# Weighted adds of gathered rows in both branches ahead of the last half copy, and a last tile that is multiplied by the norm vector ahead of its root

## The chip, the cores and the metric

The kernel runs on one core of one Trainium2 chip. The metric is the device time of one execution in microseconds (us), as the median of several runs; lower is better. The core's engines work side by side, each on its own queue, and wait for each other by semaphores: PE (TensorE, matrix products), DVE (VectorE), ACT (ScalarE), POOL (GpSimd) and SP (SyncE, which only issues transfers here).

## The reference

One decoder layer over 512 positions of 1024 channels, all in float32: a mixer (forgetting attention, a gated recurrence and a convolution side by side), cross-attention over 256 memory tokens, a mixture of experts, and a final norm. The change touches only what stands behind the experts. Each token goes to two of 16 experts, with weights w1st and w2nd; their outputs are added to the residual stream, and the sum is normed:

```python
def rmsnorm(x, g):
    y = xf * lax.rsqrt(jnp.mean(xf * xf, axis=-1, keepdims=True) + EPS)
    return (y * g.astype(jnp.float32)).astype(x.dtype)
...
    x = x + hierarchical_moe(rmsnorm(x, ffn_norm_g[l]), ...)
return rmsnorm(x, final_norm_g)
```

## The kernel before

Everything is written out by hand: each engine has its own program, and the order of its instructions is that of the code. Positions stand in four tiles t of 128 rows, `x_sb[:, t, :]` being the residual stream of a tile.

**The experts.** Tokens are sorted by expert into 12 passes p of 128 rows. For each pass, POOL gathers its rows, PE turns them, multiplies by gate and up, ACT and DVE make the hidden rows, and PE multiplies down into two banks of 512 columns. Each bank is copied to `ysb` by a `y_half(p)`: ACT the first half, DVE the second (line 1168). SP stores passes 0 to 9 to `y_dram`. Passes 10 and 11 are never stored (LATE is 2).

**The way back.** A token's two rows come back by either way. If they lie in passes 0 to 9, POOL gathers them from `y_dram` into `ygath`, eight indirect transfers in the order of tile t and of k, first or second expert (line 616). On DVE, `add_row(k, t, w)` waits for its transfer and adds the gathered rows times the weight to `x_sb` (line 1217). Rows of passes 10 and 11 come through PE: `spread_late(t)` multiplies a matrix of weights by `ysb` (line 1636), two banks for each tile. The second half of each such product needs pass 11, hence both last `y_half` copies. `add_late(t)` on DVE adds the two banks to `x_sb` (line 1224).

**Overflow.** If an expert has more than 96 tokens, a flag `over` is set, and each engine enters a branch `If` that works off what is left. With these inputs it is not entered. DVE loads the flag into a register at line 1187; the `Else` is empty. Two small instructions on `posm` (lines 1185 and 1186) prepare the overflow work ahead of it.

**The end.** For each tile ACT squares `x_sb` with a running sum (line 804, "square" below), DVE turns the sum into mean plus epsilon (`last_mean`, line 1229), POOL raises it to the power -0.5 (`final_root`, line 611), DVE multiplies `x_sb` by this root and by the norm vector `fgain` into `n_sb` (`last_norm`, line 1234), and SP stores 512 KB to the output (line 564). DVE's order is: eight add_row, then for each t add_late(t), last_norm(t-1), last_mean(t), and at the end last_norm(3).

Of the kernel before, what the change touches and what calls it, by code (L numbers as in the profile page):

```python
# [10 lines left out]
ALU = mybir.AluOpType  # L11
ACT = mybir.ActivationFunctionType
# [24 lines left out]
ST = S // P  # L37
# [30 lines left out]
NP = EX * CAP // P  # L68
# [39 lines left out]
def build(nc, x, mem, mix_norm_g, w_in, fox_f_bias, fox_norm_g, hgrn_lb_logits, hgrn_norm_g,  # L108
# [3 lines left out]
    with ExitStack() as ctx:  # L112
# [3 lines left out]
        def sem(name):  # L116
            return ctx.enter_context(nc.semaphore(name))


        x_sb = sb("x_sb", [P, ST, D])  # L120
# [285 lines left out]
        fin_ms = sem("fin_ms")  # L406
        fin_root = sem("fin_root")
        fin_out = sem("fin_out")
        half_done = sem("half_done")
        xs_step = sem("xs_step")  # L410
        root_step = sem("root_step")
# [89 lines left out]
        def experts_loads(sp):  # L501
# [59 lines left out]
                pass  # L561
            for t in range(ST):
                sp.wait_ge(fin_out, t + 1)
                sp.dma_start(out[0, t * P:(t + 1) * P, :], n_sb[:, t, :]).then_inc(out_done, 16)
            sp.wait_ge(out_done, 16 * ST)

# [178 lines left out]
        def experts_act(act):  # L745
# [56 lines left out]
            for t in range(ST):  # L802
                act.wait_ge(fin_sum, 2 * ST + 2 * t + 2)
                nc.scalar.activation(n_sb[:, t, :], x_sb[:, t, :], ACT.Square, 
                                     accum_out=ss[:, NORM0[3] + ST + t:NORM0[3] + ST + t + 1]).then_inc(fin_sq, 1)


        PROJ = ([("t", cuT[:, c], ACT.Copy) for c in range(2)] + [("t", cgT[:, c], ACT.Sigmoid) for c in range(2)]
# [197 lines left out]
        def experts_dve(dve):  # L1006
# [156 lines left out]
            def y_half(p):  # L1163
                dve.wait_ge(y_ps, 2 * p + 2)
                if p >= 2:

                    dve.wait_ge(y_stored[p % 2], 16 * (p // 2))
                nc.vector.tensor_copy(ysb[:, p % 2, 512:1024], PS[6][:, :]).then_inc(y_dve, 1)

            turned_rows(0)  # L1170
            for p in range(NP):
# [8 lines left out]
                    late_rows()  # L1180
                if 3 <= p < 3 + LATE:
                    late_turned(p - 3)
            y_half(NP - 1)

            link(nc.vector.scalar_tensor_tensor(out=posm, in0=picked, scalar=-4096.0, in1=pos, op0=ALU.mult, op1=ALU.add))
            link(nc.vector.tensor_scalar(posm, posm, 4096.0 - CAP + P, None, ALU.add))
            with dve.If(dve.value_load(over[0:1, 0:1]) > 0):
                dve.wait_ge(gu_ps, NP)
                dve.wait_ge(ht_ps, NP)
                with dve.Fori(0, OVER_PARTS) as q:  # L1190

                    nc.vector.tensor_scalar(posm, posm, -float(P), None, ALU.add).then_inc(ov_pos, 1)
                    with dve.Fori(0, EX) as e:
# [13 lines left out]
                        nc.vector.tensor_tensor(hid[:, 0], sg[:, 0], PS[2][:, FF:2 * FF], ALU.mult).then_inc(ov_hid, 1)  # L1207

                        dve.wait_ge(ov_stored, 16 * k + 16)
            with dve.Else():  # L1210
                pass

            def add_row(k, t, w):
                dve.wait_ge(fin_in[t][k], 16)
                if k:
                    dve.wait_ge(fin_sum, 2 * t + 1)
                nc.vector.scalar_tensor_tensor(out=x_sb[:, t, :], in0=ygath[:, t, k, :], scalar=w[:, t:t + 1],  # L1217
                                               in1=x_sb[:, t, :], op0=ALU.mult, op1=ALU.add).then_inc(fin_sum, 1)

            def add_late(t):  # L1220
                for n in range(2):
# [4 lines left out]
            def last_mean(t):  # L1226
                f = NORM0[3] + ST + t
                dve.wait_ge(fin_sq, t + 1)
                nc.vector.tensor_scalar(ss[:, f:f + 1], ss[:, f:f + 1], 1.0 / D, EPS, ALU.mult, ALU.add).then_inc(fin_ms, 1)

            def last_norm(t):
                f = NORM0[3] + ST + t
                dve.wait_ge(fin_root, t + 1)
                nc.vector.scalar_tensor_tensor(out=n_sb[:, t, :], in0=x_sb[:, t, :], scalar=rstd[:, f:f + 1],
                                               in1=fgain, op0=ALU.mult, op1=ALU.mult).then_inc(fin_out, 1)

            for t in range(ST):
                add_row(0, t, w1st)
                add_row(1, t, w2nd)
            dve.wait_ge(fin_sum, 2 * ST)  # L1240
            dve.wait_ge(router_in, 16 * 5)
            for t in range(ST):
                add_late(t)
                if t:
                    last_norm(t - 1)
                last_mean(t)
            last_norm(ST - 1)


        @block.vector  # L1250
# [839 lines left out]
```

## Time and profile before

| what | us |
|---|---|
| median of 3 runs | 762.64 |
| lowest and highest run | 762.08 and 763.15 |
| time of the profiled execution | 754.83 |
| its span, first to last instruction | 753.1 |
| PE busy | 697.4 |
| DVE busy | 276.1 |
| ACT busy | 146.7 |
| POOL busy | 64.9 |

The span is what the trace covers; the execution's own time is 1.7 us longer. Times in the trace are counted from the span's start. The profiled execution lies 7.8 us under the median of the runs. PE is busy for 93% of the span, but in the last 15 us it has no work left.

### The profile page before, as it was taken

To read this page: it belongs to the slowest core of one execution; us is meant where nothing else is said; L and a number is where in the kernel's file an instruction comes from. 1 tells how busy PE (TensorE), PEld (TensorE's weight loads), DVE (VectorE), ACT (ScalarE), POOL (GpSimd) and SP (SyncE) were. 2 spreads that over 40 slices of the span, in tenths; PEclk is the share of its full clock that TensorE was granted. 3 is DMA by queue.
4 is the path that set the end of the run, shared out by engine and by line. 5 is a ranking of instruction groups with operands and counts; after the bars stand their busy time and mean duration, and the time that the engine had idled before them with its cause. 6 is when DMAs were issued, how large, how long until landed. Compare 5 with 4: busy or idle time off the path is not lost.

```text
span 753.1 us, 8347 instructions
## 1 busy us (share of the span) xinstructions
PE 697.4 (93%) x3388; PEld 336.5 (45%) x3388; DVE 276.1 (37%) x646; ACT 146.7 (19%) x304; POOL 64.9 (9%) x94
## 2 busy tenths in 40 slices
PE   4999999999989999999999999999955999999992
PEld 3444745454546565454444446544442333333331
DVE  5046996533043544411220005412151732112147
ACT  3100441004262333311100003300010101011112
POOL 2000090420010000000000000000001000000031
PEclk9999999989999999999999999999985999999997
DMA  8730330302221303110009603030089799999562
GB/s 311 251 111 0 113 111 1 112 1 71 98 88 29 112 1 112 52 61 1 0 0 331 215 13 112 2 131 35 29 283 303 237 351 391 376 378 394 194 224 111
DMA packets 65714, 108.21 MB, mean 144 GB/s; under 512 B 5400, under 2 KB 40460, under 8 KB 65676
## 3 DMA queue, kind: packets, MB, share of 16 engines
q1 hardware_dynamic: 62796, 97.19, 37.0%
q0 software_dynamic: 2880, 10.49, 3.8%
q8 instruction: 27, 0.44, 0.2%
q14 instruction: 11, 0.09, 0.0%
HBM read 98.23 MB, written 9.44 MB: 143 GB/s over the span
## 4 chain that ended last, share of the span: by engine, by line
PE 88%; DVE 6%; ACT 2%; DMA 2%; issue 1%; POOL 0%; DVEq 0%; SPq 0%; POOLq 0%
PE bank L1722 27%; PE bank L1980 15%; PE bank L1587 11%; PE bank L1732 8%; PE bank L1615 6%; PE bank L1754 2%; PE bank L2053 2%; PE bank L1768 2%; PE bank L2033 2%; PE bank L1569 2%; PE bank L1924 2%; PE bank L1900 1%; DVE x_sb L1217 1%; PE bank L1533 1%; PE bank L1911 1%
## 5 line engine op out<-in xcount | busy, mean ns | idle before, releaser
L1722 PE MATMUL bank<-hT,W 128*128 128x512 f32 x384 | 168.4, 598 | 1.8 <-DVE hT L998 1.8
L1722 PEld LDWEIGHTS bank<-hT,W 128*128 128x128 f32 x384 | 72.9, 192 | 93.9 <-issue 91.3
L1980 PE MATMUL bank<-W,n_sb 128*128 128x512 f32 x256 | 111.5, 593 | 0.7 <-ACT n_sb L966 0.7
L1980 PEld LDWEIGHTS bank<-W,n_sb 128*128 128x128 f32 x256 | 48.1, 190 | 59.8 <-issue 58.3
L1587 PE MATMUL bank<-W,A 128*32 128x512 f32 x528 | 72.3, 607 | 1.5 <-DVE A L1152 1.5
L1295 DVE SCALAR_TENSOR_TENSOR A<-A,pc 128x511 f32<-128x511 f32 (+29 forms) x60 | 49.4, 824 | 2.1
L1615 PE MATMUL bank<-Dn,A 128*32 128x512 f32 x384 | 43.7, 595 | 0.5 <-ACT A L772 0.5
L1587 PE MATMUL bank<-hT,A 128*32 128x512 f32 x96 | 42.3, 594 | 0.0
L646 POOL TENSOR_TENSOR rstd<-ss,mhalf 128x1 f32<-128x1 f32 x14 | 7.7, 548 | 382.8 <-DVE ss L982 382.8
L1480 DVE TENSOR_TENSOR x_sb<-x_sb,bank 128x512 f32<-128x512 f32 x16 | 11.0, 687 | 79.7 <-PE bank L1980 79.7
L1587 PEld LDWEIGHTS bank<-W,A 128*32 128x32 f32 x528 | 19.2, 112 | 42.6 <-issue 40.4
L1722 PE MATMUL bank<-Dn,W 128*128 128x256 f32 x128 | 33.0, 416 | 4.1 <-DVE A L1452 3.9
L833 ACT ACTIVATE A<-bank 128x512 f32<-128x512 f32 (+1 forms) x22 | 12.2, 556 | 112.0 <-PE bank L1722 91.9
L1161 DVE TENSOR_TENSOR A<-A,bank 128x256 f32<-128x256 f32 x12 | 5.0, 421 | 75.6 <-ACT A L765 75.5
L1722 PEld LDWEIGHTS bank<-Dn,W 128*128 128x128 f32 x128 | 26.0, 208 | 12.4 <-DVE A L1452 8.4
L1420 DVE CUSTOM_DVE_ANT_0 hT<-bank,A 128x128 f32<-128x128 f32 (+3 forms) x32 | 14.4, 487 | 43.2 <-PE bank L1902 43.1
L1732 PE MATMUL bank<-W,hT 128*128 128x512 f32 x64 | 29.9, 623 | 0.0
L1495 DVE TENSOR_REDUCE fmx<-bank 128x1 f32<-128x256 f32 x16 | 6.7, 420 | 62.4 <-PE bank L2033 62.3
L1732 PE MATMUL bank<-W,Dn 128*128 128x512 f32 x64 | 28.2, 594 | 0.0
L743 ACT ACTIVATE A<-x_sb 128x1024 f32<-128x1024 f32 x8 | 8.5, 1057 | 95.8 <-DVE x_sb L1480 95.8
L1360 DVE SCALAR_TENSOR_TENSOR states<-states,Dn,bank 128x64 f32<-128x64 f32 x64 | 18.0, 281 | 19.7 <-PE bank L1808 17.2
L765 ACT ACTIVATE A<-bank 128x256 f32<-128x256 f32 x12 | 4.6, 384 | 100.9 <-PE bank L1587 100.9
(287 smaller groups left out, 796.2 us busy)
## 6 DMA issues: line engine op xcount, KB each, us to landing
Dn<-in_w_down_dram SPq DMA_DIRECT2D x16, 1024.0 KB, 12.3
W<-in_w_gate_dram SPq DMA_DIRECT2D x11, 1024.0 KB, 6.5
W<-in_w_up_dram SPq DMA_DIRECT2D x11, 1024.0 KB, 10.6
W<-in_w_in_dram SPq DMA_DIRECT2D x5, 2048.0 KB, 8.7
W<-in_w_xkv_dram SPq DMA_DIRECT2D x4, 2048.0 KB, 8.1
y_dram<-A SPq DMA_DIRECT2D x10, 512.0 KB, 10.9
W<-in_w_out_dram SPq DMA_DIRECT2D x2, 2048.0 KB, 7.7
W<-in_w_xq_dram SPq DMA_DIRECT2D x2, 2048.0 KB, 8.4
```

What stands on the lines that cost most here:

```text
L1295: nc.vector.scalar_tensor_tensor(out=y[:, s:S], in0=a[:, 0:S - s], scalar=pc[:, r:r + 1], in1=y[:, s:S], op0=ALU.mult, op1=ALU.add).then_i ...
L1360: nc.vector.scalar_tensor_tensor(out=states[:, k + 1, :], in0=states[:, k, :], scalar=he4[:, p, k * CHUNK + CHUNK - 1:k * CHUNK + CHUNK], ...
L1569: mm = nc.tensor.transpose(PS[k][:, c * P:(c + 1) * P], src[:, b, (4 * k + c) * P:(4 * k + c + 1) * P], identf[:, :])
L1587: mm = nc.tensor.matmul(PS[2 + b][r, :], xgT[:, b, c, r], gu_at[GU_HOME[e]][:, c, :], start=c == 0, stop=c == DC - 1)
L1615: mm = nc.tensor.matmul(PS[5 + n][r, :], hidT[:, p % 2, k, r], Dn[:, DN_HOME[e], k, 512 * n:512 * n + 512], start=k == 0, stop=k == 1)
L1722: mm = nc.tensor.matmul(bank[0:w, 0:n], lhs, src[:, c, 0:n], start=c == 0, stop=c == DC - 1)
L1732: mm = nc.tensor.matmul(bank[:, 0:w], src[:, c, t * P:(t + 1) * P], W[:, slot, c, col:col + w], start=c == 0, stop=c == DC - 1)
L1754: mm = nc.tensor.matmul(bank[:, 0:IW], hT[:, c, t * P:(t + 1) * P], w_if[:, c, :], start=c == 0, stop=c == DC - 1)
L1768: mm = nc.tensor.matmul(bank[:, :], lhs, hT[:, c, :], start=c == 0, stop=c == DC - 1)
L1924: mm = nc.tensor.matmul(PS[6][64 * a:64 * a + 64, i * P:(i + 1) * P], v[:, j, h * FD:(h + 1) * FD], fpT[a][:, j * P:(j + 1) * P], start=j ...
L1980: mm = nc.tensor.matmul(PS[k % 4][:, :], src[:, c, t * P:(t + 1) * P], W[:, (n_load + n) % SLOTS, c, :], start=first and j == 0, stop=last ...
L2033: mm = nc.tensor.matmul(PS[u % 2][:, 0:M], xqT[:, 2 * h + k, t * P:(t + 1) * P], xkT[:, 2 * h + k, :], start=k == 0, stop=k == 1)
```

## The change

- The two small instructions on `posm` and the load of the flag stand right behind the copy of pass 10. The copy of pass 11 on DVE, `y_half(NP - 1)`, moves into both branches.
- The eight `add_row` move into both branches. In the branch without overflow, those of tile 0 stand ahead of the copy of pass 11, the six others behind it.
- The tail's order is add_late(t), last_mean(t-1), last_norm(t-2). For the last tile, DVE first multiplies `x_sb` by `fgain` into `x_gain`, a part of `A` whose gathered rows are used up, without waiting for the root. When the root is there, DVE multiplies the first 512 columns by it, and ACT the last 512 (a copy with a scale).
- SP waits for both halves before it stores the last tile. The number of stores stays four.

```diff
--- before.py
+++ after.py
@@ -406,6 +406,8 @@
         fin_ms = sem("fin_ms")
         fin_root = sem("fin_root")
         fin_out = sem("fin_out")
+        fin_gain = sem("fin_gain")
+        fin_act = sem("fin_act")
         half_done = sem("half_done")
         xs_step = sem("xs_step")
         root_step = sem("root_step")
@@ -561,6 +563,8 @@
                 pass
             for t in range(ST):
                 sp.wait_ge(fin_out, t + 1)
+                if t == ST - 1:
+                    sp.wait_ge(fin_act, 1)
                 sp.dma_start(out[0, t * P:(t + 1) * P, :], n_sb[:, t, :]).then_inc(out_done, 16)
             sp.wait_ge(out_done, 16 * ST)
 
@@ -803,6 +807,11 @@
                 act.wait_ge(fin_sum, 2 * ST + 2 * t + 2)
                 nc.scalar.activation(n_sb[:, t, :], x_sb[:, t, :], ACT.Square, 
                                      accum_out=ss[:, NORM0[3] + ST + t:NORM0[3] + ST + t + 1]).then_inc(fin_sq, 1)
+            f = NORM0[3] + ST + t
+            act.wait_ge(fin_gain, 1)
+            act.wait_ge(fin_root, ST)
+            act.wait_ge(fin_sq, ST)
+            nc.scalar.activation(n_sb[:, t, 512:1024], A[:, 512:1024], ACT.Copy, scale=rstd[:, f:f + 1]).then_inc(fin_act, 1)
 
 
         PROJ = ([("t", cuT[:, c], ACT.Copy) for c in range(2)] + [("t", cgT[:, c], ACT.Sigmoid) for c in range(2)]
@@ -1180,11 +1189,18 @@
                     late_rows()
                 if 3 <= p < 3 + LATE:
                     late_turned(p - 3)
-            y_half(NP - 1)
+
+            def add_row(k, t, w):
+                dve.wait_ge(fin_in[t][k], 16)
+                if k:
+                    dve.wait_ge(fin_sum, 2 * t + 1)
+                nc.vector.scalar_tensor_tensor(out=x_sb[:, t, :], in0=ygath[:, t, k, :], scalar=w[:, t:t + 1],
+                                               in1=x_sb[:, t, :], op0=ALU.mult, op1=ALU.add).then_inc(fin_sum, 1)
 
             link(nc.vector.scalar_tensor_tensor(out=posm, in0=picked, scalar=-4096.0, in1=pos, op0=ALU.mult, op1=ALU.add))
             link(nc.vector.tensor_scalar(posm, posm, 4096.0 - CAP + P, None, ALU.add))
             with dve.If(dve.value_load(over[0:1, 0:1]) > 0):
+                y_half(NP - 1)
                 dve.wait_ge(gu_ps, NP)
                 dve.wait_ge(ht_ps, NP)
                 with dve.Fori(0, OVER_PARTS) as q:
@@ -1207,15 +1223,16 @@
                         nc.vector.tensor_tensor(hid[:, 0], sg[:, 0], PS[2][:, FF:2 * FF], ALU.mult).then_inc(ov_hid, 1)
 
                         dve.wait_ge(ov_stored, 16 * k + 16)
+                for t in range(ST):
+                    add_row(0, t, w1st)
+                    add_row(1, t, w2nd)
             with dve.Else():
-                pass
-
-            def add_row(k, t, w):
-                dve.wait_ge(fin_in[t][k], 16)
-                if k:
-                    dve.wait_ge(fin_sum, 2 * t + 1)
-                nc.vector.scalar_tensor_tensor(out=x_sb[:, t, :], in0=ygath[:, t, k, :], scalar=w[:, t:t + 1],
-                                               in1=x_sb[:, t, :], op0=ALU.mult, op1=ALU.add).then_inc(fin_sum, 1)
+
+                for t in range(ST):
+                    add_row(0, t, w1st)
+                    add_row(1, t, w2nd)
+                    if t == 0:
+                        y_half(NP - 1)
 
             def add_late(t):
                 for n in range(2):
@@ -1234,17 +1251,23 @@
                 nc.vector.scalar_tensor_tensor(out=n_sb[:, t, :], in0=x_sb[:, t, :], scalar=rstd[:, f:f + 1],
                                                in1=fgain, op0=ALU.mult, op1=ALU.mult).then_inc(fin_out, 1)
 
-            for t in range(ST):
-                add_row(0, t, w1st)
-                add_row(1, t, w2nd)
             dve.wait_ge(fin_sum, 2 * ST)
             dve.wait_ge(router_in, 16 * 5)
             for t in range(ST):
                 add_late(t)
                 if t:
-                    last_norm(t - 1)
-                last_mean(t)
-            last_norm(ST - 1)
+                    last_mean(t - 1)
+                if t >= 2:
+                    last_norm(t - 2)
+            x_gain = A[:, 0:1024]
+            dve.wait_ge(fin_sum, 4 * ST)
+            nc.vector.tensor_tensor(x_gain, x_sb[:, t, :], fgain, ALU.mult).then_inc(fin_gain, 1)
+            last_mean(t)
+            last_norm(t - 1)
+            dve.wait_ge(fin_gain, 1)
+            dve.wait_ge(fin_root, ST)
+            f = NORM0[3] + ST + t
+            nc.vector.tensor_scalar(n_sb[:, t, 0:512], x_gain[:, 0:512], rstd[:, f:f + 1], None, ALU.mult).then_inc(fin_out, 1)
 
 
         @block.vector
```

DVE's program, from the copies of the last two passes to the first instruction inside the overflow branch; `bank6` is the bank of the second half, TENSOR_LOAD is the flag's load. Before:

```order
L1168 COPY A<-bank6 128x512 x2
L1185 SCALAR_TENSOR_TENSOR A<-A 128x64
L1186 TENSOR_SCALAR A<-A 128x64
L1187 TENSOR_LOAD A
L1187 COMPARE_AND_BRANCH
```

Now:

```order
L1177 COPY A<-bank6 128x512
L1200 SCALAR_TENSOR_TENSOR A<-A 128x64
L1201 TENSOR_SCALAR A<-A 128x64
L1202 TENSOR_LOAD A
L1202 COMPARE_AND_BRANCH
L1177 COPY A<-bank6 128x512
```

Only one copy is left ahead of the load; the other stands first in the overflow branch here (the row behind the branch), and once more in the other branch. The next rows are DVE's again, from the end of the overflow branch to the first late add (bank0). Before:

```order
L1190 REGISTER_ALU
L1190 COMPARE_AND_BRANCH
L1187 UNCONDITIONAL_BRANCH
L1217 SCALAR_TENSOR_TENSOR x_sb<-W,A,x_sb 128x1024 x8
L1224 TENSOR_TENSOR x_sb<-x_sb,bank0 128x512
```

Now:

```order
L1197 SCALAR_TENSOR_TENSOR x_sb<-W,A,x_sb 128x1024 x8
L1202 UNCONDITIONAL_BRANCH
L1197 SCALAR_TENSOR_TENSOR x_sb<-W,A,x_sb 128x1024 x2
L1177 COPY A<-bank6 128x512
L1197 SCALAR_TENSOR_TENSOR x_sb<-W,A,x_sb 128x1024 x6
L1229 UNCONDITIONAL_BRANCH
L1241 TENSOR_TENSOR x_sb<-x_sb,bank0 128x512
```

The eight adds of the first row belong to the overflow branch. Without overflow the program goes on behind the first unconditional branch: two adds, the copy, six adds, and one more unconditional branch. Last, DVE's end, from the late adds of tile 2 (bank4 and bank7) on. Before:

```order
L1224 TENSOR_TENSOR x_sb<-x_sb,bank4 128x512
L1224 TENSOR_TENSOR x_sb<-x_sb,bank7 128x512
L1234 SCALAR_TENSOR_TENSOR n_sb<-x_sb,rstd,A 128x1024
L1229 TENSOR_SCALAR ss<-ss 128x1
L1224 TENSOR_TENSOR x_sb<-x_sb,bank5 128x512
L1224 TENSOR_TENSOR x_sb<-x_sb,bank6 128x512
L1234 SCALAR_TENSOR_TENSOR n_sb<-x_sb,rstd,A 128x1024
L1229 TENSOR_SCALAR ss<-ss 128x1
L1234 SCALAR_TENSOR_TENSOR n_sb<-x_sb,rstd,A 128x1024
```

Now, from the late adds of tile 2 on:

```order
L1241 TENSOR_TENSOR x_sb<-x_sb,bank4 128x512
L1241 TENSOR_TENSOR x_sb<-x_sb,bank7 128x512
L1246 TENSOR_SCALAR ss<-ss 128x1
L1251 SCALAR_TENSOR_TENSOR n_sb<-x_sb,rstd,A 128x1024
L1241 TENSOR_TENSOR x_sb<-x_sb,bank5 128x512
L1241 TENSOR_TENSOR x_sb<-x_sb,bank6 128x512
L1246 TENSOR_SCALAR ss<-ss 128x1
L1251 SCALAR_TENSOR_TENSOR n_sb<-x_sb,rstd,A 128x1024
L1264 TENSOR_TENSOR A<-x_sb,A 128x1024
L1246 TENSOR_SCALAR ss<-ss 128x1
L1251 SCALAR_TENSOR_TENSOR n_sb<-x_sb,rstd,A 128x1024
L1270 TENSOR_SCALAR n_sb<-A,rstd 128x512
```

Each mean and norm stands one tile later than before, and the last norm of 128x1024 has become a product of 128x1024 ahead of the last mean and a half product of 128x512 at the very end.

## Rows read from the trace of the kernel before

**Rows 1.** The page: busy tenths in 40 slices; shares of the chain.
```profile
PE   4999999999989999999999999999955999999992
DVE  5046996533043544411220005412151732112147
...
PE 88%; DVE 6%; ACT 2%; DMA 2%; issue 1%; POOL 0%; DVEq 0%; SPq 0%; POOLq 0%
```

**Rows 2.** DVE's timeline: start us, length us, line, operation [idle before <- releaser].
```profile
720.90 0.69 DVE L1168 COPY A<-bank 128x512 f32<-128x512 f32 x1 [2.60 <-PE bank L1615]
725.39 0.69 DVE L1168 COPY A<-bank 128x512 f32<-128x512 f32 x1 [3.79 <-PE bank L1615]
...
727.29 10.44 DVE L1217 SCALAR_TENSOR_TENSOR x_sb<-W,A,x_sb 128x1024 f32<-128x1024 f32 x8 [0.85 <-DVE A L1186]
737.76 1.29 DVE L1224 TENSOR_TENSOR x_sb<-x_sb,bank 128x512 f32<-128x512 f32 x2
740.26 0.15 DVE L1229 TENSOR_SCALAR ss<-ss 128x1 f32<-128x1 f32 x1 [1.21 <-ACT n_sb L804]
...
745.45 1.27 DVE L1224 TENSOR_TENSOR x_sb<-x_sb,bank 128x512 f32<-128x512 f32 x2
746.64 1.28 DVE L1234 SCALAR_TENSOR_TENSOR n_sb<-x_sb,rstd,A 128x1024 f32<-128x1024 f32 x1
747.94 0.15 DVE L1229 TENSOR_SCALAR ss<-ss 128x1 f32<-128x1 f32 x1
748.75 1.28 DVE L1234 SCALAR_TENSOR_TENSOR n_sb<-x_sb,rstd,A 128x1024 f32<-128x1024 f32 x1 [0.66 <-POOL rstd L611]
```

**Rows 3.** The chain of waits, its branch: start us, length us, what.
```profile
727.05 0.07 DVEq L1187
```

**Rows 4.** PE's late product in the timeline, and one window with the granted clock.
```profile
725.25 14.09 PE L1636 MATMUL bank<-A 128*128 128x512 f32 x32
...
727.00:738.00 11.00, 11.00 (x27) 4.86 (x26) 10.25 (x9) 0.00 (x0) 0.00 (x0) 1.00 0.12 50
```

**Rows 5.** POOL's gathers, first and last of eight; their landing; DMA at 728.
```profile
714.29 0.94 POOL L616 DMA_INDIRECT W<-y_dram,A  x1 [30.56 <-DMA y_dram<-A]
...
722.99 0.93 POOL L616 DMA_INDIRECT W<-y_dram,A  x1 [0.30 <-issue]
...
DMA to landing us min/median/max: 5.6/7.4/7.5
...
728.00:729.00 1.00, 1.00 (x4) 0.50 (x3) 0.89 (x2) 0.00 (x0) 0.00 (x0) 1.00 0.29 115
```

**Rows 6.** Timeline, two small adds on DVE, and POOL's indirect issue.
```profile
596.59 0.23 DVE L1120 TENSOR_TENSOR A<-A 128x64 f32<-128x64 f32 x1
...
597.36 0.23 DVE L1123 TENSOR_TENSOR A<-A 128x64 f32<-128x64 f32 x1
...
596.80 0.94 POOL L606 DMA_INDIRECT A<-n_dram,A  x1 [8.31 <-PE bank L1569]
```

**Rows 7.** Groups by shape: busy us, mean ns of one.
```profile
L1429 DVE TENSOR_SCALAR hT<-hT,frr 128x512 f32<-128x512 f32 x8 | 3.9, 486 | 0.3
...
L1137 DVE TENSOR_TENSOR states<-states,A 128x512 f32<-128x512 f32 x2 | 1.4, 692 | 0.1
...
L914 ACT ACTIVATE A<-n_sb 128x512 f32<-128x512 f32 x4 | 2.5, 616 | 7.6 <-DVE n_sb L1441 7.6
```

**Rows 8.** The stores of the output: issues on SP, and their landing.
```profile
L564 SPq DMA_DIRECT2D out_dram<-n_sb x4: 332/332/333, 742.8 to 750.1; - x4
...
DMA to landing us min/median/max: 2.6/2.6/2.6
```

**Rows 9.** Windows after the last store's issue; DMA share and GB/s stand last.
```profile
750.07:750.85 0.78, 0.00 (x0) 0.00 (x0) 0.00 (x0) 0.00 (x0) 0.00 (x0) 0.50 0.01 0
750.85:752.25 1.40, 0.00 (x0) 0.00 (x0) 0.00 (x0) 0.00 (x0) 0.00 (x0) 0.50 0.92 375
```

## The prediction

> **What bounds the kernel now.** I read the page's chain of work first: 88% of it is PE, 6% is DVE [rows 1]. So a change on DVE can count only where DVE ends the chain, and the slices show one such place: the last fortieth (18.8 us), where PE falls to 2 tenths and DVE rises to 7. Next the timeline of DVE over that stretch [rows 2]. It reads as one string. The copy of pass 10 starts at 720.90 and lasts 0.69; then DVE is idle for 3.79 us until PE's last down product lets the copy of pass 11 start at 725.39; 1.90 us after it the first weighted add starts (727.29), eight adds take 10.44 (2.61 for a pair), the first two late adds start at 737.76, and from there to the last norm at 748.75 DVE stands still twice, 1.21 us for the first square and 0.66 us for the last root. The reader is to see the hole of 3.79 us in front of 10.44 us of adds, and that these adds lie in the chain. The 1.90 us hold the copy, two tiny instructions, the load of the flag, and a branch that starts at 727.05, takes 0.07 and is followed by the add 0.17 us later [rows 2, 3].
>
> Then what DVE could have been waiting for. PE's late product runs from 725.25 for 14.09 us, to 739.34, at a granted clock of 1.00, that is 2.4 GHz [rows 4]; the late adds start only at 737.76, and the very last of them, second of the two from 745.45, starts at about 746.05 [rows 2], so PE has slack of 6.7 us. The gathers are issued by POOL from 714.29 to 722.99 and land 5.6 to 7.5 us later; DMA's share is down to 0.29 at 728 to 729, so the last has landed by 729 [rows 5]. The first landed at 719.9 (714.29 + 5.6, the shortest), at the latest 721.8 (with 7.5); the second was issued 1.24 later, so at the latest 723.0. Two of them lie ready while DVE is idle.
>
> **Part 1, two adds into the hole.** In the new order the tiny instructions, the flag and the branch come behind the copy of pass 10, so the first add starts at 720.90 + 1.90 = 722.80, its rows being there. The pair takes 2.61: the last copy can start at 725.41, against 725.39 before. That is nothing for PE, which waits for this copy ahead of the second half of its late product: I move PE's end from 739.34 to 739.4. The six other adds start 0.61 after the copy and take 6 x 1.305 = 7.83: they end at 725.41 + 0.61 + 7.83 = 733.85, not at 737.73. Their rows: with 7.5 us to land, rows 3 and 4 are there by 725.5 (needed at 726.0 and 727.3), 5 and 6 by 728.0 (728.6, 729.9), 7 and 8 by 730.5 (731.2, 732.6). Margins are 0.5 us and more by this worst case, so I cost the gathers at nothing. The adds save 3.9 us.
>
> **Part 2, the jump behind the adds.** The branch "no overflow" now has a body, and its end jumps to the very next instruction. No unconditional jump shows in the trace. From below it costs nothing; from above I take a whole DMA, 2.6 us from issue to landing [rows 8], as if the instructions had to be fetched. The nearest row is the taken branch: 0.07 and 0.17 behind it [rows 3]. I take 0.15: the late adds start at 734.00. The Trainium skill (Runtime: NRT & Kernel Launch, Instruction fetch mechanics) says that a taken branch stalls when its target lies outside the two instruction pages held. By that rule a stall is possible at both jumps; the row here shows that a jump over 30 instructions of DVE's program did not stall, and the new ones go 44 and 1 forward.
>
> **Part 3, the new order of the last tiles.** I follow DVE with the steps of rows 2: two late adds 1.19 (745.45 to 746.64), a mean 0.07 when its square is there, a norm 1.20 when the next does not wait for it (1.28 less the overlap of 0.08), 1.30 up to a mean behind it (746.64 to 747.94); a square's mean comes 1.18 after the square starts (the first late adds end at 737.76 + 1.29 = 739.05, the square follows them by 0.03, its mean starts at 740.26).
> - Late adds 0 at 734.00, 1 at 735.19; mean 0 waits for its square: 735.32 + 1.18 = 736.50. Late adds 2 at 736.57, mean 1 at 737.76, norm 0 at 737.83.
> - Late adds 3 at 739.03, the second of them at 739.63. PE is done at 739.4: the slack that was 6.7 us is now 0.2 us. Mean 2 at 740.22, norm 1 at 740.29.
> - The product with the norm vector at 741.49. Its form, a tensor_tensor of 128x1024 from SBUF, is not in the trace: 128x512 took 0.692 [rows 7], twice that is 1.38; the three-operand form of that size took 1.28 [rows 2]. It is nearest to the second, and I take 1.30 to the next start (bounds 1.2 and 1.4). Mean 3 needs the square of tile 3 by then: 740.25 + 1.21 = 741.5, there in time.
> - Mean 3 at 742.79, its root ready 0.81 later (747.94 to 748.75 before) at 743.60, hidden by norm 2 at 742.86 to 744.14. Then the last half: 128x512 with a scalar from SBUF took 0.486 [rows 7]; the end is 744.14 + 0.49 = 744.6 (0.07 less if the overlap holds). ACT's half starts when the root is ready and takes 0.616 [rows 7], over at 744.25, so it hides.
> DVE ended at 748.75 + 1.28 = 750.03 before. The sum on DVE is -5.4 us.
>
> **Part 4, the stores collide.** Before, the four stores followed norms 2.5 us apart and each landed 2.6 us after its issue. A store moves its data in about 1.3 us (0.92 of 1.40 us) after 0.8 us with no traffic, and lands about 0.5 us after the data [rows 8, 9]. Now the third is issued at 744.17, the fourth at 744.65. The third's data go from 744.97 to 746.27, the fourth's behind it to 747.57, landing at 748.1, not 744.65 + 2.6 = 747.25. Bounds: 0 and 0.85 us given back; the share of 0.92 says that one store fills the engines, so I take 0.85. The last landing moves from 750.07 + 2.6 = 752.67 to 748.1: **-4.6 us**.
>
> Sum: span 753.1 - 4.6 = 748.5, the profiled execution 754.83 - 4.6 = 750.3. The median of the runs is 7.8 us above that execution; nothing in the trace says where, so I carry the difference over: 762.64 - 4.6 = **758.1**. Its own range, by the bounds: 757.0 (stores do not collide, jump free, product 1.2) to 759.3 (product 1.4, jump 0.24, and a us of gathers or of PE).
>
> **Rivals.**
> - *Instruction fetch at the jumps.* For it: the trace has no unconditional jump inside these streams, and both jumps are on DVE's string. Against: rows 3. Price 2.6 us for one: 760.7; both, 763.3. Chance 8% for one, 2% for both.
> - *POOL holds the port.* The first adds read two operands from SBUF at 722.80, while POOL still issues gathers until 723.92 [rows 5]. If one had to wait, the add would start 1.12 us late and push the copy, PE and the rest by as much: 759.2. Against: a tensor_tensor with two SBUF inputs took 0.23 at 596.59 and 0.23 at 597.36, the second inside an indirect issue at 596.80 to 597.74 [rows 6]. Chance 4%. The Trainium skill (SBUF — State Buffer, Who interferes with whom) says that such a DVE instruction contends with a GpSimd one that reads SBUF; by that the time would be 759.2, and the rows of the small ones speak against it here.
> - *The rows of tile 0 come late.* The copy of pass 11 is now queued behind two adds that wait for gathers, and PE behind the copy. The second add wants its rows at 724.1; if they landed 2.6 us after that, at 726.7, everything would come 2.6 us later: 760.7. Their latest landing here is 723.0, so they would have to be 3.7 us later than in this trace. In executions of 762 us, transfers may be later than in this one. Chance 4%.
> - *PE becomes the bound, the one that ends slower.* Slack is 0.2 us now. Late by x, PE costs the new order x - 0.2, the old one only x - 6.7. Past x = 4.8 the new order loses, and past x = 6.7 its tail behind the last late add decides: 744.6 - 739.63 = 4.97 against 750.03 - 746.05 = 3.98 us, and 0.85 for the stores, so +1.8 us: 764.5. It takes a late product of over 20 us in place of 14.09, a clock near 1.2 GHz for half of it. Rows 4 have 1.00 throughout. Chance 3%.
> - *The change does not do what it says:* the adds still start behind the copy because the flag's load waits for something else. In rows 2 and 3 nothing but the 1.90 us lies between copy and add, and the flag was written long before. Then part 3 and 4 stand alone, 758.1 + 3.9 = 762.0. Chance 2%.
>
> **How the numbers follow.** The cases above leave 77% to the forecast. A difference under 0.2% (1.5 us) is about what a measurement of this kernel can't tell from none. Faster: the forecast, the port, late rows, one fetch, 93%, of which I keep back 5% for what the unexplained 7.8 us may hide: 0.88. Same: both fetches, no effect, part of what I kept back: 0.08. Slower: PE and the remainder: 0.04. The range of 8 in 10 starts at the lower bound of the forecast, 757.0, and reaches to one fetch or late rows, 760.7.
>
> **What the new profile would show.** First add near 722.8, copy of pass 11 within 0.1 us of 725.4, PE's late product of 14.1 us ending near 739.4; DVE's late adds from 734.0, hardly a gap up to 744.6; the last two stores 0.5 us apart with the last landing over 3 us after its issue. It is wrong if DVE stands idle behind either jump, if the first add or the copy starts over 0.5 us late, or if PE releases the last late add.

## The result and the profile after

The changed kernel takes 756.7 us in the median (752.91 to 759.51, 20 runs). The kernel before, run again beside it, takes 761.84 us (757.71 to 765.66, 20 runs, the first three among them), so those three, at 762.64, had been a little high. The ratio is 0.9934, with a 95% interval of 0.9919 to 0.995: 5.0 us less, between 3.8 and 6.2. The ratios here and below are worked out over the runs and lie up to 0.23% from the quotient of the two medians. The 4.6 us of the sum lie in that interval. The predicted time does not hold: 756.7 is 0.3 us below the range of 757.0 to 760.7.

The profiled execution of the changed kernel took 759.51 us, its span 757.8, which is longer than the 753.1 of before. It must not be compared whole against whole, and the first thing to read is why. Its timeline of DVE, in the manner of [rows 2]: start us, length us, line, operation, and in brackets the idle time before it with what ended it.

```profile
728.08 0.69 DVE L1177 COPY A<-bank 128x512 f32<-128x512 f32 x1 [7.51 <-remote]
...
729.99 2.69 DVE L1197 SCALAR_TENSOR_TENSOR x_sb<-W,A,x_sb 128x1024 f32<-128x1024 f32 x2 [0.85 <-DVE A L1201]
734.51 0.69 DVE L1177 COPY A<-bank 128x512 f32<-128x512 f32 x1 [1.84 <-PE bank L1638]
735.12 7.83 DVE L1197 SCALAR_TENSOR_TENSOR x_sb<-W,A,x_sb 128x1024 f32<-128x1024 f32 x6
742.99 2.48 DVE L1241 TENSOR_TENSOR x_sb<-x_sb,bank 128x512 f32<-128x512 f32 x4
...
746.81 1.28 DVE L1251 SCALAR_TENSOR_TENSOR n_sb<-x_sb,rstd,A 128x1024 f32<-128x1024 f32 x1
748.01 1.28 DVE L1241 TENSOR_TENSOR x_sb<-x_sb,bank 128x512 f32<-128x512 f32 x2
...
749.26 1.28 DVE L1251 SCALAR_TENSOR_TENSOR n_sb<-x_sb,rstd,A 128x1024 f32<-128x1024 f32 x1
750.46 1.22 DVE L1264 TENSOR_TENSOR A<-x_sb,A 128x1024 f32<-128x1024 f32 x1
751.59 0.15 DVE L1246 TENSOR_SCALAR ss<-ss 128x1 f32<-128x1 f32 x1
752.12 1.28 DVE L1251 SCALAR_TENSOR_TENSOR n_sb<-x_sb,rstd,A 128x1024 f32<-128x1024 f32 x1 [0.38 <-POOL rstd L615]
753.32 0.48 DVE L1270 TENSOR_SCALAR n_sb<-A,rstd 128x512 f32<-128x512 f32 x1
```

Two things differ in kind from what was foreseen. The first is ahead of the edit: the copy of pass 10 waits 7.51 us, where it waited 2.60 in [rows 2], and the copy of pass 11 comes 6.43 us behind it instead of 4.49. That the unchanged kernel can show it too is seen below. The second is inside the tail: norm 2 waits 0.38 us for its root.

A stretch that leaves the first out runs from the start of the copy of pass 11 to the end of the span: 753.1 - 725.39 = 27.71 us before, 757.8 - 734.51 = 23.29 us now, **4.42 us less**, where the prediction had 4.57. Over all profiles of one kernel below it repeats to 0.05 us, so it tells differences that the runs' medians, with an interval of some 0.2% either way, can't.

PE's timeline in the same execution shows its two last products, and the stores of the output answer to [rows 8].

```profile
728.56 5.88 PE L1638 MATMUL bank<-Dn,A 128*32 128x512 f32 x32 [5.09 <-ACT A L776]
734.37 14.10 PE L1659 MATMUL bank<-A 128*128 128x512 f32 x32
```

```profile
L568 SPq DMA_DIRECT2D out_dram<-n_sb x4: 332/333/368, 748.1 to 753.9; - x4
...
DMA to landing us min/median/max: 2.6/2.6/3.5
```

The late product ends at 748.47; the second late add of tile 3 starts 0.6 behind 748.01, so PE is 0.1 us ahead of it and holds nothing up. One store of the four lands 3.5 us after its issue; it is the last, since 753.9 + 3.5 = 757.4, and 0.4 us behind its landing the span ends, as it did before. The third is issued 0.45 us ahead of it, at 753.43.

### The profile page after: what moved, and what is told of

It reads as the page before. It is cut to its first block, busy times and chain, and to the rows that moved or that the text cites. A ratio compares the mean times of both kernels' runs of the same rounds, so it can differ in the third digit from the quotient of the medians.

```text
span 757.8 us, 8352 instructions
## 1 busy us (share of the span) xinstructions
PE 701.1 (93%) x3388; PEld 337.8 (45%) x3388; DVE 276.2 (36%) x647; ACT 147.4 (19%) x305; POOL 68.2 (9%) x94
## 4 chain that ended last, share of the span: by engine, by line
PE 88%; DVE 5%; DMA 2%; ACT 2%; issue 1%; POOL 1%; another core or an unknown queue 1%; DVEq 0%; SPq 0%; POOLq 0%
PE bank L1745 26%; PE bank L2003 15%; PE bank L1610 11%; PE bank L1755 8%; PE bank L1638 6%; PE bank L1777 2%; PE bank L2076 2%; PE bank L1791 2%; PE bank L2056 2%; PE bank L1592 2%; PE bank L1947 2%; PE bank L1923 1%; PE bank L1912 1%; PE bank L1556 1%; PE bank L1934 1%; PE bank L1850 1%
## 5 line engine op out<-in xcount | busy, mean ns | idle before, releaser
L1638 PE MATMUL bank<-Dn,A 128*32 128x512 f32 x384 | 45.9, 621 | 5.1 <-ACT A L776 5.1
L1638 PEld LDWEIGHTS bank<-Dn,A 128*32 128x32 f32 x384 | 11.9, 114 | 30.9 <-issue 25.6
```

The source lines that it names most:

```text
L1638: mm = nc.tensor.matmul(PS[5 + n][r, :], hidT[:, p % 2, k, r], Dn[:, DN_HOME[e], k, 512 * n:512 * n + 512], start=k == 0, stop=k == 1)
```

## The experiments

### One half of the change at a time

The kernel before once more, unchanged, as a measure of the noise: 

> The kernel before against itself: ratio 1.000 within 0.2%. Theory A (the tail alone moved): its stretch from the start of DVE's last y_half copy to the landing of the last store is 27.3 us as before. Theory B (the 7.8 us between the first profile of before and its median sit in one stretch, seen in the profile of the changed kernel as idle time of PE around passes 10 and 11): this profile shows the same idle time of 4 to 5 us between the hidden transposes of pass 11 and the last down product, and the execution lies at 758 us or above.

Measured: 761.22 us (12 runs) against 760.40 for before (35 runs), 0.9988 [0.9966, 1.0011]; the stretch is 27.70 us, as in the first profile. But this profile, too, has the late copies:

```profile
726.21 0.69 DVE L1168 COPY A<-bank 128x512 f32<-128x512 f32 x1 [7.43 <-remote]
732.80 0.69 DVE L1168 COPY A<-bank 128x512 f32<-128x512 f32 x1 [5.90 <-PE bank L1615]
```

So the unchanged kernel shows them as well, and they are no effect of the edit. What follows compares the stretch, which starts behind them.

The adds alone, with the tail of before (cut from the diff of the change: what leaves its old place, and what stands in the branch without overflow instead):

```
-            y_half(NP - 1)
...
+                for t in range(ST):
+                    add_row(0, t, w1st)
+                    add_row(1, t, w2nd)
+                    if t == 0:
+                        y_half(NP - 1)
...
-            for t in range(ST):
-                add_row(0, t, w1st)
-                add_row(1, t, w2nd)
```

> The moved adds with the old tail. Prediction's sum: adds -3.9, jump +0.15, stores free: -3.7 us, ratio 0.995. Rival (the gain comes from the tail): under 1.5 us. In the profile: last y_half copy to last landing 23.5 us; late adds right behind the six adds; POOL's roots 0.55 us each except where they lie under a norm.

Measured: 757.67 us, 0.9961 [0.994, 0.9982]; the stretch is 23.82, **3.88 us less** than 27.70.

The new tail alone, with the adds where they were before (the reverse of that diff, applied to the changed kernel):

> The new tail with the adds where they were. Prediction's sum: 5.4 - 3.9 = 1.5 less on DVE, 0.85 given back by the stores: -0.7 us, ratio 0.999. Theory of the port (a root on POOL cannot run while DVE reads two operands from SBUF): -0.7 + 0.46 = -0.2 us, root of tile 2 over 2 us long. Rival (the tail is worth 1.5 in full): ratio 0.998. Stretch from the last copy to the last landing 26.6 (no port) or 27.1 (port).

Measured: 760.03 us, 0.9993 [0.9971, 1.0015], no difference by the runs; the stretch is 27.15, **0.55 us less**. The two halves add up, 3.88 + 0.55 = 4.43 against 4.42 for the whole change. So nearly nine tenths of the gain is the hole filled with adds, and the rearranged tail, with its product and its split, is worth half a us. The stretch alone does not decide between the two theories on record for this run: up to the last landing it is 26.8 us, where 26.6 stood for no port and 27.1 for the port. The length of a root does. Here are all four, on POOL (same columns):

```profile
747.57 0.57 POOL L615 TENSOR_TENSOR rstd<-ss,mhalf 128x1 f32<-128x1 f32 x1 [23.40 <-DVE ss L1238]
748.82 1.52 POOL L615 TENSOR_TENSOR rstd<-ss,mhalf 128x1 f32<-128x1 f32 x1 [0.68 <-DVE ss L1238]
751.27 3.17 POOL L615 TENSOR_TENSOR rstd<-ss,mhalf 128x1 f32<-128x1 f32 x2 [0.93 <-DVE ss L1238]
```

The four roots are all the same instruction on 128x1 numbers. Root 0 takes 0.57 us, root 1 takes 1.52, and roots 2 and 3 together 3.17; cut apart in the changed kernel's own trace, root 2 is 2.65:

```profile
749.43 2.65 POOL L615 TENSOR_TENSOR rstd<-ss,mhalf 128x1 f32<-128x1 f32 x1 [0.93 <-DVE ss L1246]
```

Lay it beside DVE's rows above. It starts under norm 1 (749.26 to 750.54), the product with the norm vector follows that without a gap (750.46 to 751.68), and the root is ready at 752.08, 0.40 us behind the product. In the old order three roots lay under late adds, whose second operand is a bank of PSUM, and the last under no work of DVE; there each took 0.55 to 0.57. Roots 1 and 2 both start 0.17 us behind the start of a norm, which reads two operands from SBUF, and seem to stand still until such work ends. Root 3 does not: it starts at 752.06, 0.06 us ahead of norm 2, and takes 0.54 us with that norm running over it, while the norm keeps its 1.28. So the overlap by itself is not enough; here only a root that came behind the norm's start was long. The next two runs test what DVE's operand has to do with it.

### Moving the root, and moving DVE's operand

Mean 2 goes between the two halves of tile 3's late adds, so that root 2 lies under an add from PSUM:

```
-                add_late(t)
-                if t:
+                if t == ST - 1:
+                    add_late(t, (0,))
...
+                    add_late(t, (1,))
```

(between the two calls, "..." is the mean of tile t - 1)

> The changed kernel with the mean of tile 2 between the two half adds of tile 3, so that its root starts 0.6 us earlier, under an add that reads PSUM. Theory of the port: root of tile 2 takes 0.55 us instead of 2.65, norm 2 starts without the wait of 0.38, and the root of tile 3 now falls under norm 2 and is long instead: the stretch from copy to landing is 22.84 us less 0.1 to 0.4. Rival (the root was long because POOL was slow there, whatever DVE did): root 2 still over 2 us. Against the kernel before: ratio 0.993 to 0.994.

Measured: 757.12 us, 0.9956 [0.9933, 0.9979]; the stretch is 22.73, 0.56 less than the changed kernel's. Root 2 falls to 0.55 us, and now root 3 is the one that starts behind a norm, by 0.16 us:

```profile
743.58 0.55 POOL L615 TENSOR_TENSOR rstd<-ss,mhalf 128x1 f32<-128x1 f32 x1 [0.33 <-DVE ss L1246]
746.57 1.52 POOL L615 TENSOR_TENSOR rstd<-ss,mhalf 128x1 f32<-128x1 f32 x1 [2.44 <-DVE ss L1246]
```

```profile
746.41 1.27 DVE L1251 SCALAR_TENSOR_TENSOR n_sb<-x_sb,rstd,A 128x1024 f32<-128x1024 f32 x1
748.20 0.49 DVE L1275 TENSOR_SCALAR n_sb<-A,rstd 128x512 f32<-128x512 f32 x1 [0.51 <-POOL rstd L615]
```

Root 3 ends at 748.09, 0.41 behind the norm's end at 747.68, and the last half waits 0.51 us for it. The 0.56 us are therefore not the wait that was taken away. Counted from the copy of pass 11, the last store is issued later than in the changed kernel (748.98 - 729.27 = 19.71 against 753.88 - 734.51 = 19.37 us), but the third goes out 1.27 us ahead of it instead of 0.45, and all four land about 2.6 us after their issue. The stores gave 0.9 us back, and the new wait took 0.34. (Up to the last landing the stretch is 22.35; expected was 22.44 to 22.74, for the removed wait.)

The other way to take the operand away: ACT copies the norm vector into two free banks of PSUM, and norms 1 and 2 and the product read it there, in halves of 512:

```
+                if t == 2:
+                    for n in range(2):
+                        nc.scalar.activation(PS[n][:, :], fgain[:, 512 * n:512 * n + 512], ACT.Copy).then_inc(y_act, 1)
...
+                        mm = nc.vector.scalar_tensor_tensor(out=n_sb[:, t, h], in0=x_sb[:, t, h], scalar=rstd[:, f:f + 1],
+                                                            in1=PS[n][:, :], op0=ALU.mult, op1=ALU.mult)
```

> The changed kernel, its order kept, but norms 1 and 2 and the product of tile 3 read the norm vector from two PSUM banks (copied there by ACT after the square of tile 2), in halves of 512, so that DVE reads one operand from SBUF. Theory of the port: roots of tiles 2 and 3 take 0.55 us though DVE works all the time; norm 2 starts without its 0.38 us wait; stretch from the last copy to the span's end 22.8 to 22.9 us instead of 23.3. Rival (a root is long under any DVE work): root 2 over 2 us, stretch 23.3 or more for the added instructions.

Measured: 750.73 us against 755.26 for before (34 runs, one of which, at 4065.83 us, is left out of the ratio), 0.9946 [0.9924, 0.9968]; the stretch is 23.12. DVE is busy throughout, and yet:

```profile
736.43 1.53 POOL L615 TENSOR_TENSOR rstd<-ss,mhalf 128x1 f32<-128x1 f32 x1 [0.68 <-DVE ss L1249]
738.89 0.55 POOL L615 TENSOR_TENSOR rstd<-ss,mhalf 128x1 f32<-128x1 f32 x1 [0.93 <-DVE ss L1249]
741.46 0.55 POOL L615 TENSOR_TENSOR rstd<-ss,mhalf 128x1 f32<-128x1 f32 x1 [2.02 <-DVE ss L1249]
```

```profile
736.27 1.28 DVE L1263 SCALAR_TENSOR_TENSOR n_sb<-x_sb,rstd,A 128x1024 f32<-128x1024 f32 x1
...
738.72 1.40 DVE L1259 SCALAR_TENSOR_TENSOR n_sb<-x_sb,rstd,bank 128x512 f32<-128x512 f32 x2
740.04 1.28 DVE L1280 TENSOR_TENSOR A<-x_sb,bank 128x512 f32<-128x512 f32 x2
741.23 0.15 DVE L1249 TENSOR_SCALAR ss<-ss 128x1 f32<-128x1 f32 x1
741.30 1.40 DVE L1259 SCALAR_TENSOR_TENSOR n_sb<-x_sb,rstd,bank 128x512 f32<-128x512 f32 x2
```

Root 1 still lies under norm 0, which reads SBUF twice, and takes 1.53; roots 2 and 3 lie under norms that read a bank, and take 0.55. These norms come in two halves, but root 2 is over at 739.44, before the first half ends at 739.46, so it waited for no end of an instruction; what is left is the place of the operand. The wait is gone, but a norm in two halves costs 1.32 us to the next start instead of 1.20, and the product 1.19 instead of 1.13. So only 0.17 us of the stretch is gained, and 23.12 misses the 22.8 to 22.9 that was expected.

### The stores

The third store of the changed kernel is left out (its 128 rows of the output stay unwritten, and SP's last wait counts three stores):

```
+                if t != ST - 2:
+                    sp.dma_start(out[0, t * P:(t + 1) * P, :], n_sb[:, t, :]).then_inc(out_done, 16)
```

> The changed kernel without the store of tile 2 (its rows of the output are left unwritten). Prediction's term (the last store's data wait behind the third's, 0.85 us): the last store lands 2.6 us after its issue instead of 3.5, stretch from the last copy to the span's end 22.4 instead of 23.3 us. Rival (stores overlap and the 3.5 us have another cause): 3.5 us and 23.3 us stay.

Measured: 751.86 us in a single run; the stretch is 22.35, 0.94 less than 23.29, and the stores land at one pace:

```profile
DMA to landing us min/median/max: 2.6/2.6/2.6
```

So the collision of the last two stores costs 0.9 us, as part 4 had it (0.85).

### The late copies

Two theories had been left for them: that PE waits for instructions, which would have to do with where its program is in them or with the gathers that crowd them out; or that it belongs to the chip. First the gathers of the kernel before, thinned to 64 of 1024 columns (the other columns of the gathered rows are not brought):

```
-                        nc.gpsimd.indirect_dma_start(out=ygath[:, t, k, :], out_offset=None, in_=written,
+                        nc.gpsimd.indirect_dma_start(out=ygath[:, t, k, 0:64], out_offset=None, in_=written.rearrange("r (c n) -> (r c) n", n=64),
```

> The kernel before, its eight gathers of the way back moving 64 of 1024 columns of each row (the rest of the gathered rows is left as it lay there, so the output is not the reference's). Theory of the congestion (PE's last down products end late because the gathers fill the DMA engines from 714 to 729): the late end of pass 10's down product is gone, last copy but one 3.7 us after that product's start instead of 8.5, PE's clock does not fall, and the time goes down by 5 to 8 us, ratio 0.990 to 0.993. Rival (it has another cause): ratio 0.999 to 1.001, the copy again 8.5 us after.

Measured: 754.05 us against 754.71 for before (21 runs), 0.9988 [0.9972, 1.0003]. No late copies; but before itself took 5.7 us less here than the 760.40 beside the runs above.

Then 50 tiny products at the start of PE's program in the changed kernel, which shift every instruction behind them:

```
+            for _ in range(50):
+                nc.tensor.matmul(PS[1][:, 0:8], identf[:, :], identf[:, 0:8], start=True, stop=True)
```

> The changed kernel with 50 tiny products at its start, 200 instructions more on PE, under PE's first wait; they shift where in the program PE crosses the pages in which its instructions are fetched. Theory of the fetch (a page of PE's instructions, fetched while the gathers fill the DMA engines, holds PE up around pass 10): no late end of pass 10's down product, ratio to the kernel before 0.984 to 0.988. Rival (congestion or another cause): the late end stays, ratio 0.993 to 0.996, as the changed kernel.

Measured: 769.51 us, 1.0177 [1.0149, 1.0206], where 0.984 to 0.988 or 0.993 to 0.996 had been expected, because the products did not hide under PE's first wait but took 21.50 us of PE behind it:

```profile
4.28 21.50 PE L1731 MATMUL bank<-identf 128*128 128x8 f32 x100 [4.28 <-DMA mixrow<-in_mix_norm_g_dram]
```

The stretch was 23.30 and the copies were not late. The changed kernel itself went along in that session:

> The changed kernel again: ratio 0.9934 within 0.2%, stretch from the last copy to the span's end 23.3 us within 0.1, late end of pass 10's down product as in four of the five profiles taken since the first.

Measured: 751.12 us, 0.9953 [0.9934, 0.9972], 3.6 us less than 754.71; the stretch is 23.29 again. Its copies are not late either, so the thinned gathers and the shifted program prove nothing: there was nothing for them to cure. The two controls were repeated once more beside the version of the next part.

> The kernel before with thin gathers (64 of 1024 columns moved, output not the reference's) once more, beside a profile of the kernel before on the same chip. Tells something only if that profile has the late end of pass 10's down product. Congestion by the gathers: it is gone with thin gathers, 7 us less. Another cause: both have it, ratio 0.999. If neither has it, the late end belongs to the chip and not to the program.

> The kernel before against itself: ratio 1.000 within 0.2%; stretch from the last copy to the span's end 27.7 us within 0.05. Whether DVE's copy of pass 10 comes 3.7 or 8.5 us after the start of PE's down product says which kind of chip this is: 754 us for the first, 760 for the second.

Measured: 754.40 us, 0.9993 [0.9967, 1.0018], and 755.02 us, 1.0000 [0.9979, 1.0022], stretches of 27.75 both, no late copies in either.

The windows over the end of the down products show what the late copies are. The changed kernel's first profile (PE's busy time first; granted clock, DMA share and GB/s last):

```profile
724.00:725.00 1.00, 0.00 (x0) 0.00 (x0) 0.00 (x0) 0.30 (x1) 0.94 (x1) 1.00 0.90 344
...
726.00:727.00 1.00, 0.00 (x0) 0.00 (x0) 0.00 (x0) 0.00 (x0) 0.18 (x1) 0.65 1.00 385
727.00:728.00 1.00, 0.00 (x0) 0.00 (x0) 0.00 (x0) 0.00 (x0) 0.00 (x0) 0.50 1.03 397
728.00:729.00 1.00, 0.44 (x4) 0.20 (x8) 0.88 (x3) 0.38 (x1) 0.00 (x0) 0.50 1.01 393
```

PE stands still for 5.09 us, ACT for 3.83 and DVE for 7.51, instead of 0.47, 1.46 and 2.60, while the gathers fill the DMA engines; the clock granted to PE falls from 1.00 to 0.50, that is from 2.4 to 1.2 GHz, after PE has been idle, and stays there until the window of 733, so that the last down product takes 5.88 us instead of 3.64. In the unchanged kernel's second profile the copy of pass 10 waits 7.43 us instead of 2.60 and that of pass 11 comes 6.59 behind it instead of 4.49: 4.8 + 2.1 = 6.9 us. All four profiles of one session, on one chip (before, adds only, tail only, early mean), have this, none of the eight of two later sessions on another chip has, before and changed kernels alike, and the medians of before are 760.4 in the one and 754.7 and 755.3 in the others. In the profiled execution of before that the prediction read, the copies were not late, while the three runs beside it were 7.8 us longer. **That is where most of the 7.8 us lie**, as far as these runs tell: late copies account for 6.9 of them. The medians of the sessions are only 5.1 to 5.7 us apart, so the account does not close. Whether the chip or the session decides can't be told apart, since the first chip had only one session; and what releases the copies (the trace names no engine of this core) stays open.

Three rows narrow it. A full load of the DMA engines is not enough: in the changed kernel's second profile they are busy at 1.05 and 414 GB/s in the window 726 to 727, with PE at 1.00. The lateness starts while the clock still stands at 1.00: ACT's copy of the first half of pass 10 comes 4.22 us behind the start of its down product (723.70 - 719.48) instead of 1.97 (719.57 - 717.60). And one block of 16 KB on the trace's instruction queue falls into this stretch. In the kernel before with thinned gathers its transfer begins 0.03 us ahead of the copy of pass 10, both times; with full gathers and no late copies 1.6 to 2.6 us behind it (six profiles, the shifted program not counted); and in the five profiles with late copies within 0.4 us of it, at 727.73 against 728.08 in the first of the changed kernel and at 726.10 against 726.21 in the second of the unchanged one. So the gathers do hold up that transfer, and where the copies are late it begins just as they are released. Whether it releases them is not shown.

### A version from the pieces

Early mean, norm vector in PSUM for norms 1 and 2 and the product, norms 1 and 2 ahead of the product, and the last tile split 640 to 384 columns between DVE and ACT:

```
-            nc.vector.tensor_scalar(n_sb[:, t, 0:512], x_gain[:, 0:512], rstd[:, f:f + 1], None, ALU.mult).then_inc(fin_out, 1)
+            nc.vector.tensor_scalar(n_sb[:, t, 0:640], x_gain[:, 0:640], rstd[:, f:f + 1], None, ALU.mult).then_inc(fin_out, 1)
```

> As the run before, with the mean of tile 2 between the half adds of tile 3, mean 3 and norm 2 ahead of the product of tile 3, and 640 columns of the last tile on DVE, 384 on ACT. Port and store theories together: no wait for a root, the third store out 1.7 us ahead of the fourth so that both land 2.6 us after their issue: stretch 21.9 us (23.3 - 0.46 - 0.85), ratio to the kernel before 0.992 (5.8 us). Rival (the stores' term was something else): 22.7 as with the early mean alone.

Measured: 749.52 us against 755.26, 0.9936 [0.9916, 0.9957]; the stretch is 22.42, 0.87 less than the changed kernel's. Its last two stores no longer collide: all four land 2.6 us after their issue. It beats the kernel before by 4.8 us by the ratio, 5.7 by the medians. Against the changed kernel the runs don't separate it: they were not run beside one another here, and the intervals, 0.9953 [0.9934, 0.9972] and this one, overlap. The stretch says that it is shorter by 0.9 us, the early mean alone by 0.56. That 0.9 is the stores' term and nothing else: the third goes out at 742.12 and the fourth at 744.02, which is 19.44 us behind the copy of pass 11 against 19.37 in the changed kernel. Expected was 21.9; what the wait for the root had cost went into the halves.

## Why the prediction was right in its steps and wrong in its number

**The step that failed** is the last of the sum: "The median of the runs is 7.8 us above that execution; nothing in the trace says where, so I carry the difference over: 762.64 - 4.6". The median of three runs was taken for the level of the kernel, with no term in the range for how well three runs give it. With 20 runs beside the changed kernel it is 761.84, and 761.84 - 4.6 = 757.2 would have been in the range. In another session, on another chip, it is 754.7. The miss of 1.4 us (758.1 - 756.7) is thus 0.8 of level and 0.5 or so of difference: 5.1 by the medians against 4.6. The stretch has 4.42, so that 0.5 is no gain that a profile shows, and it lies within the interval. The range had bounds for jumps, stores and products of a few tenths of a us each and none for a level that moves by 0.8 us between two samplings, and by 5.1 to 5.7 us between sessions on different chips. How three runs can mislead shows in the 20 of the changed kernel. Fourteen of them lie in three groups by the clock granted over the execution: 753.05 to 754.40 in four runs at 0.975, 755.62 to 756.15 in four at 0.970, 758.26 to 759.51 in six at 0.966. What sorts a run into its group stays open. A forecast of the difference was sound; the absolute number stood on the weakest row.

**Part 1 was right**, to 0.02 us: -3.9 foreseen, -3.88 with the adds alone. The adds start 1.91 behind the copy of pass 10 (729.99 - 728.08), as it took from [rows 2]. Where the copies are not late, the copy of pass 11 follows 4.53 behind that of pass 10; foreseen was 725.41 - 720.90 = 4.51. The six adds take 7.83.

**Part 2 was too dear**: the late adds start at 742.99, the six adds end at 742.95. The unconditional jump costs 0.01 us more than the same joint in [rows 2], not 0.15, and the jump into the branch costs 0.01 to 0.03 beyond the old 1.90. No fetch of 2.6 us shows, on either chip. The rule of the Trainium skill (Runtime: NRT & Kernel Launch, Instruction fetch mechanics) is that a taken branch stalls when its target lies outside the two instruction pages held; neither jump stalled, so no run here shows that rule at work.

**Part 3 had two terms off, of opposite sign.** Norm 2 was to follow mean 3 after 0.07; it follows after 0.53 (752.12 - 751.59), so 0.46 us was lost to root 2. The product was 1.30 to the next start; it is 1.13, 0.17 gained. Their sum is the difference between the 0.84 that parts 2 to 4 would have given alone (4.57 + 0.15 - 3.88) and the 0.55 that they gave: 0.46 - 0.17 = 0.29.

**Part 4 was right**: last landing 3.5 us after issue where 3.45 was foreseen, and 0.94 us back without the third store. With the third and fourth stores 1.27 and 1.90 us apart (early mean, last version) the 0.9 us are gone as well.

**The rival "POOL holds the port" was looked for at the wrong place, and on the wrong side.** It was set against the first adds, with DVE as the one that waits, and given 4% because of [rows 6]. In the five profiles of the new order without late copies, the first add and the last gather do meet. DVE and POOL in the changed kernel's second profile:

```profile
723.21 2.68 DVE L1197 SCALAR_TENSOR_TENSOR x_sb<-W,A,x_sb 128x1024 f32<-128x1024 f32 x2 [0.85 <-DVE A L1201]
```

```profile
722.13 0.94 POOL L620 DMA_INDIRECT W<-y_dram,A  x1 [0.31 <-issue]
723.37 1.93 POOL L620 DMA_INDIRECT W<-y_dram,A  x1 [0.30 <-issue]
```

The pair of adds takes its usual time. It is the gather's issue that doubles, 1.93 us instead of 0.94, in each of these five profiles, and never where it meets no add. It does not wait for both adds: it ends at 725.30, 0.81 us behind the first add's end at 724.49, while the second, which starts 0.12 us after that end, runs to 725.89. Its rows are wanted last, so nothing follows here. In the tail POOL's wait has a price: roots 1 and 2 take 1.52 and 2.65 us, with 0.46 us of it on the path. That POOL pays is shown by the early mean (2.65 to 0.55 us) and by the norm vector in PSUM (DVE as busy as ever, root 0.55). The Trainium skill (SBUF — State Buffer, Who interferes with whom) states that a DVE instruction with two SBUF inputs contends with a GpSimd instruction that reads SBUF. The trace agrees, at 2.65 us against 0.55, and shows who waits: each time POOL, whose instruction started 0.16 or 0.17 us behind DVE's. Root 2 is held over norm and product, which overlap by 0.08 us; the gather's issue gets through where 0.12 us lie between two adds. Root 3, started 0.06 us ahead of its norm, is not held at all. The rule was weighed for one pair only; it should have been held against every root, since the edit moved roots 1 and 2 from under late adds to under norms.

**PE as the bound** did not come, at 0.1 us of slack: the late product took 14.09 to 14.14 us in every profile, on either chip, although the down product ahead of it ran at 1.2 GHz on one of them. **Late rows of tile 0** did not come either; the copy of pass 11 is never held up by an add that waits.

## What to carry to other kernels

Forecast the difference, and give the absolute number a range that holds the spread of the level between samplings, and between sessions on different chips; when the profiled execution and the median lie 1% apart, that gap is a finding of its own and not an offset to carry. Before moving work on DVE, list what POOL does under each of its instructions that read two SBUF operands, in the new order and not the old; a result that POOL must deliver belongs under work whose second operand is in PSUM. When moving a wait changes the end of a kernel, look at the spacing of its last stores before crediting the wait: of the early mean's 0.56 us none came from the shorter root. Look for a hole in front of independent work first: filling it gave 3.9 us, rearranging an already dense tail 0.55.

## What the hardware showed that was not expected

- The length of a GpSimd instruction on 128 numbers depends on DVE: 0.55 us alone or under PSUM operands, 1.52 when it starts 0.17 us behind one norm of 1.28 us, 2.65 behind a norm and a product back to back, ending 0.40 us behind them, but 0.54 when it starts 0.06 us ahead of the norm. An indirect issue that starts behind an add takes 1.93 us instead of 0.94.
- In one session PE stands still for 5.0 to 5.1 us and ACT for 3.8 beside saturated DMA, and PE's clock falls from 2.4 to 1.2 GHz after it, 6.9 us in all; in two sessions on another chip, with DMA as full, the same program does not.
- Two stores of 512 KB issued 0.45 us apart land 2.6 and 3.5 us after their issue; issued 1.27 us apart, 2.6 us both.
- A product with 8 columns at the start of the program took 21.50 / 100 = 0.215 us a record, at a granted clock of 1.00.
